# A reordered first stage: c as a row, modulation tiles between the halves of x, chunks split one by one, and products of ones in TensorE's early waits

## The reference, cut to what matters

```python
mod = (jax.nn.silu(c) @ ada_w + ada_b).reshape(bsz, DEPTH, 2, 3, D_MODEL)
shift, scale, gate = (mod[:, i, 0, k][:, None, :] for k in range(3))
h = rmsnorm(x, norm_g[i, 0]) * (1.0 + scale) + shift
# rmsnorm(x, g) = x * rsqrt(mean(x * x) + EPS) * g
b_gate, c_gate, v = jnp.split(h @ w_in, 3, axis=-1)      # a_in
u = causal_depthwise_conv(c_gate * v, conv_w)
return (b_gate * u) @ w_out                              # a_out
```

## Time and profile before

| | |
|---|---|
| time, median of 3 runs | 2176.7 us (2174.73 to 2178.79) |
| the profiled execution: its time, its span | 2175.51 us, 2173.7 us |
| TensorE busy | 2121.2 us (98%) |
| VectorE, ScalarE, POOL busy | 55%, 45%, 45% |
| TensorE idle for ScalarE's `h_hi`, whole run | 15.9 us |
| idle of TensorE before its first product | 12.9 us |
| mean granted clock | 0.998 |

### The profile page before, as it was taken

The page is one execution under the profiler, slowest core; times in us unless marked ns, Lnnn a source line. Parts: engine busy times, 40 slices in busy tenths (PEclk is TensorE's granted clock), DMA queues, the critical chain, the costliest instruction groups (busy, mean ns, idle before and its releaser), DMA issues.

```text
span 2173.7 us, 28374 instructions
## 1 busy us (share of the span) xinstructions
PE 2121.2 (98%) x10264; PEld 1720.5 (79%) x10264; DVE 1194.1 (55%) x1709; ACT 971.6 (45%) x1405; POOL 973.1 (45%) x421
## 2 busy tenths in 40 slices
PE   5999999999999999999999999999999899999998
PEld 4788888888887777778888888887776688888886
DVE  7876666412377788876422221421878745666522
ACT  5224522234455556654544333544555644444332
POOL 3544544456543333335544456564221243444563
PEclk9999999999999999999999999999999999999999
DMA  8663656733344443523233323255211132333232
GB/s 331 238 243 104 223 219 251 220 96 97 101 133 141 142 141 120 177 60 110 87 96 96 88 80 99 91 152 156 71 62 49 46 100 88 96 96 96 80 99 72
DMA packets 74477, 274.33 MB, mean 126 GB/s; under 512 B 8647, under 2 KB 11335, under 8 KB 67992
## 3 DMA queue, kind: packets, MB, share of 16 engines
q1 hardware_dynamic: 71016, 267.29, 37.7%
q10 hardware_dynamic: 3376, 5.90, 0.8%
HBM read 269.76 MB, written 8.12 MB: 128 GB/s over the span
## 4 chain that ended last, share of the span: by engine, by line
PE 73%; issue 14%; POOL 5%; DVE 5%; ACT 1%; DMA 1%; SPq 0%; ACTq 0%; POOLq 0%; DVEq 0%
PE bank L560 62%; POOL wlo L521 5%; PE bank L930 4%; PE bank L1022 2%; PE bank L951 1%; PE bank L987 1%; DVE x L1583 1%; PE bank L970 1%; PE bank L623 1%; DMA raw<-a_in_d 1%; DVE sq L1579 1%; DVE ada_first L1609 1%; PE bank L871 1%; DVE ta L1557 0%; DVE stat L1984 0%
## 5 line engine op out<-in xcount | busy, mean ns | idle before, releaser
L521 POOL TENSOR_TENSOR wlo<-raw,whi 128x1024 fp32r<-128x1024 f32 x382 | 927.7, 2436 | 1127.0 <-ACT whi L1060 1127.0
L1060 ACT ACTIVATE whi<-raw 128x1024 fp32r<-128x1024 f32 x382 | 399.8, 1055 | 570.1 <-PE bank L560 549.0
L560 PE MATMUL bank<-h_hi,whi 128*128 128x512 f32 x1608 | 630.9, 392 | 2.6 <-POOL wlo L521 2.6
L560 PE MATMUL bank<-h_hi,wlo 128*128 128x512 f32 x1608 | 626.2, 389 | 0.0
L560 PE MATMUL bank<-h_lo,whi 128*128 128x512 f32 x1608 | 625.7, 389 | 0.0
L560 PEld LDWEIGHTS bank<-h_hi,whi 128*128 128x128 f32 x1608 | 301.9, 188 | 69.6 <-issue 6.3
L560 PEld LDWEIGHTS bank<-h_hi,wlo 128*128 128x128 f32 x1608 | 301.8, 188 | 63.7
L560 PEld LDWEIGHTS bank<-h_lo,whi 128*128 128x128 f32 x1608 | 302.0, 188 | 61.7
L560 PE MATMUL bank<-g_hi,whi 128*128 128x512 f32 x592 | 230.3, 389 | 0.0
L560 PE MATMUL bank<-g_lo,whi 128*128 128x512 f32 x592 | 230.3, 389 | 0.0
L560 PE MATMUL bank<-g_hi,wlo 128*128 128x512 f32 x592 | 230.3, 389 | 0.0
(11 more groups left out here) (339 smaller groups left out, 2815.5 us busy)
## 6 DMA issues: line engine op xcount, KB each, us to landing
raw<-f_in_d SPq DMA_DIRECT2D x88, 512.0 KB, 3.6
raw<-m_d SPq DMA_DIRECT2D x65, 512.0 KB, 3.7
ada_f<-ada_d SPq DMA_DIRECT2D x24, 1024.0 KB, 6.8
raw<-g_in_d SPq DMA_DIRECT2D x44, 512.0 KB, 3.6
raw<-w_in_d SPq DMA_DIRECT2D x41, 512.0 KB, 3.6
csb<-cs_d SPq DMA_DIRECT2D x32, 640.0 KB, 5.7
ada_a<-ada_d SPq DMA_DIRECT2D x16, 1024.0 KB, 5.1
raw<-a_in_d SPq DMA_DIRECT2D x24, 512.0 KB, 6.6
```

The source lines that it names most:

```text
L521: nc.gpsimd.tensor_tensor(wlo[:, s], raw[:, s], whi[:, s].bitcast(F32), ALU.subtract).then_inc(lo_ready, 1)
L560: mm = nc.tensor.matmul(psum[bank][:], w[:, s, kk, :], xs[part == "lo"][:, k, :], start=first and kk == 0 and i == 0, stop=last and kk == ...
L1060: nc.scalar.activation(whi[:, s], raw[:, s], ACT.Copy).then_inc(hi_ready, 1)
```

## The change

It reorders the first stage; the arithmetic of all later stages stays.

- SyncE issues c first, as one row of 4 KB; then half of x, the first 160 columns of `vec`, modulation tile 0, the other half of x, `kst`, and the chunks 0 to 3 each with the tile after it. The rest of `vec` comes behind tile 7 and has a wait of its own.
- TensorE lays c over the partitions with two products of one row of ones, and ScalarE takes silu in place. A copy of silu(c) is kept in `cond` behind the last norm tile; before f_in0 this copy is copied back to PSUM in place of silu computed anew.
- The squares go to eight buffers (`y`), three sums are made of them (k = 0 to 3, 4 and 5, 6 and 7), and `token_sums` adds the three in PSUM.
- VectorE does tile 0's columns between the first and second half of the squares, tile 1's before the reciprocal; the 128 x 1 scale goes to ScalarE (`first_scale`).
- ScalarE converts chunk 0 before the root, chunk 1 after it, chunk 2 before k = 1 and chunk 3 before k = 2. POOL takes `wlo(0)`, `wlo(1)`, `h_lo(0)`, `wlo(2)`, `h_lo(1)`, `wlo(3)`, `h_lo(2)` and so on.
- TensorE takes in `four` for a_in tiles 0 and 1 first, tile 2 for k = 0 to 2 once chunk 2 is split, tile 3 likewise, and from k = 3 as before.
- `keep_warm(5, n)`, n products of 128 columns of ones to an unused bank, stand before and between the early waits.

```diff
+            sp.dma_start(cond[0:1].rearrange("p a n -> p (a n)"), io["c"]).then_inc(c_in, 16)
+            x_half(0)
+            sp.dma_start(vec[:, 0:VFIRST], io["vec"][:, 0:VFIRST]).then_inc(vec_in, 16)
             ada_start(0)
+            x_half(1)
             sp.dma_start(kst[:], io["kst"]).then_inc(kst_in, 16)
-            load(io["a_in"][0], 0)
-            ada_start(1)
-            for v in range(1, 4):
+            for v in range(4):
                 load(io["a_in"][v], v)
                 ada_start(v + 1)
             for k in range(5, KD):
                 ada_start(k)
+            sp.dma_start(vec[:, VFIRST:NV], io["vec"][:, VFIRST:NV]).then_inc(vec_in, 16)
...
+            split_lo(0)
+            for k in range(3):
+                split_lo(k + 1)
+                low_part("a_in", k)
+            for k in range(3, KD - 1):
+                low_part("a_in", k)
...
+                    turn(0, (0, 1))
+                    turn(1, (0, 1))
+                    for k in range(3):
+                        turn(k, (2,))
+                    turn(2, (0, 1))
+                    for k in range(3):
+                        turn(k, (3,))
+                    for k in range(3, KD - 2):
+                        turn(k, range(4))
...
-                pe.wait_ge(row_acc, KD - 1)
-                token_sums(4, rstd[:], True).then_inc(s_done, 1)
+                for i, k in enumerate(ROW_SUMS):
+                    pe.wait_ge(row_acc, i + 1)
+                    mm = token_sums(4, y[:, k, :], i == 0)
+                    if i == 0:
+                        keep_warm(5, 6)
+                mm.then_inc(s_done, 1)
             pe.wait_ge(const_ready, 1)
+            keep_warm(5, 8)
+            pe.wait_ge(c_in, 16)
+            for a in range(2):
+                mm = nc.tensor.matmul(psum[6 + a][:], ones[0:1, :], cond[0:1, a, :], start=True, stop=True)
+            mm.then_inc(c_rows, 1)
+            keep_warm(5, 6)
             first_root()
+            keep_warm(5, 4)
             pe.wait_ge(kst_in, 16)
             spread(4, 0, R1)
+            keep_warm(5, 6)
             four("a_in", 0)
...
+            def first_scale(k):
+                if k in (1, 2):
+                    split_hi(k + 1)
+                act.wait_ge(col_out, k + 1)
+                g = V("norm_g", k)
+                nc.scalar.activation(ncol[:, 0, 0, k:k + 1], mod[:, KD + k:KD + k + 1], ACT.Identity, bias=g, scale=g).then_inc(ncol_ready, 1)
+                act.wait_ge(ncol_ready, k + 1)
...
+            first_squares(0)
+            act.wait_ge(c_rows, 1)
+            nc.scalar.activation(silu_c, silu_c, ACT.Silu).then_inc(c_ready, 1)
             set_root()
+            first_squares(1)
+            split_hi(0)
             act.wait_ge(s_done, 1)
             take_root(0, token_sum(4))
+            split_hi(1)
             act.wait_ge(vec_in, 16)
+            mod_norm(0, "a_in", 0, first_scale)
+            act.wait_ge(c_ready, 1)
+            nc.scalar.activation(cond[:], silu_c, ACT.Copy).then_inc(c_kept, 1)
+            act.wait_ge(vec_in, 32)
...
-            condition()
+            act.wait_ge(c_kept, 1)
+            nc.scalar.activation(silu_c, cond[:], ACT.Copy).then_inc(c_ready, 1)
...
+            first_cols(0)
+            for k in (4, 6):
+                dve.wait_ge(sq_out, k + 2)
+                TT(y[:, k, :], y[:, k, :], y[:, k + 1, :], ALU.add).then_inc(row_acc, 1)
+            first_cols(1)
+            dve.wait_ge(std_out, 1)
+            nc.vector.tensor_copy(ssum[:], token_sum(4))
+            inverse(0, R1)
+            dve.wait_ge(rb_done, 1)
             for k in range(KD):
+                if k >= 2:
+                    first_cols(k)
                 scaled(k, 4, 0, "a_in")
             low("a_in")
+            dve.wait_ge(vec_in, 32)
```

More of the change, by code:

```diff
@@ L95 @@
 V0, NV = starts(VCOLS)
+VFIRST = V0["a_conv"]
 KCOLS = dict(ident=128, tri=128, qvalid=4, emask=2)
@@ L530, in splits, with low_part @@
                     split_lo(c)
+            def low_part(phase, k):
+                pool.wait_ge(in_hi, I0[phase] + k + 1)
+                nc.gpsimd.tensor_tensor(h_lo[:, k, :], tb[:, k % 2, :], h_hi[:, k, :].bitcast(F32),
+                                        ALU.subtract).then_inc(in_ready, 1)
             def low(phase):
                 for k in range(KD - 1):
[L535 to L540, removed]
+                    low_part(phase, k)
+            split_lo(0)
[4 more added lines that the diff above has]
+                low_part("a_in", k)
+            first = RING
+            for phase in BY_TILE[1:]:
                 splits(first, C0[phase] + RING)
@@ L600, in turn @@
                         lower(i, k)
-                for k in range(KD - 2):
-                    turn(k, range(4))
+                if n:
+                    for k in range(KD - 2):
+                        turn(k, range(4))
+                else:
+                    turn(0, (0, 1))
[6 more added lines that the diff above has]
+                    for k in range(3, KD - 2):
+                        turn(k, range(4))
                 turn(KD - 2, (0, 1))
@@ L1094, in x_root, with norm_out @@
                 take_root(X_ROOT[i], token_sum(4))
-            def norm_out(i, phase, a, b):
+            def norm_out(i, phase, a, b, ahead=None):
                 for k in range(KD):
-                    if i == 0:
-                        act.wait_ge(ncol_ready, k + 1)
+                    if ahead is not None:
+                        ahead(k)
                     act.wait_ge(t_out, KD * i + k + 1)
@@ L1140, in y_tile, with first_squares @@
                 split_hi(c + RING + chunks - 1)
[L1142 to L1155 removed]
+            def first_squares(h):
+                act.wait_ge(x_in[h], 16)
+                for k in range(4 * h, 4 * h + 4):
+                    nc.scalar.activation(y[:, k, :], x[:, k, :], ACT.Square).then_inc(sq_out, 1)
+            def first_scale(k):
[5 more added lines that the diff above has]
+                act.wait_ge(ncol_ready, k + 1)
+            act.wait_ge(const_ready, 1)
+            nc.scalar.activation(root[:, SPARE, 1:2], epscol[:], ACT.Silu)
+            first_squares(0)
+            act.wait_ge(c_rows, 1)
+            nc.scalar.activation(silu_c, silu_c, ACT.Silu).then_inc(c_ready, 1)
             set_root()
+            first_squares(1)
+            split_hi(0)
             act.wait_ge(s_done, 1)
             take_root(0, token_sum(4))
[L1159 to L1160 removed]
+            split_hi(1)
             act.wait_ge(vec_in, 16)
[L1162 removed]
+            mod_norm(0, "a_in", 0, first_scale)
+            act.wait_ge(c_ready, 1)
+            nc.scalar.activation(cond[:], silu_c, ACT.Copy).then_inc(c_kept, 1)
+            act.wait_ge(vec_in, 32)
             for j in range(8):
@@ L1619, in first_cols @@
             def first_cols(k):
[L1621 to L1625, removed]
+                dve.wait_ge(first_in[k], 16)
+                mod_col(k, ada_first[k][:, 0])
+                mod_col(KD + k, ada_first[k][:, 1]).then_inc(col_out, 1)
             def scale_col(q):
```

33 lines of the change are left out of this document (12 added, 21 removed).

## The result

The changed kernel takes 2170.9 us (median of 12 runs, 2169.8 to 2172.7) beside 2176.8 for the kernel before (12 runs, 2174.7 to 2179.0): the ratio is 0.9973, 95% interval 0.9966 to 0.9981. The forecast was 2171.9 in a range from 2169.2 to 2175.4. The profiled execution has a span of 2168.3 us, before 2173.7.

What follows compares the result with a forecast made beforehand. Only the program's start could be shortened, held by the fourth chunk's transfer, then VectorE. Reordering ends the first four tiles at 48.2 instead of 53.05 us, a gain of 4.8 from the 2176.7 median: 2171.9 us, range 2169.2 to 2175.4.

Steps and rivals of the forecast that it cites:

- What holds the start: First stage before the change: the fourth weight chunk's transfer until 26.2, then VectorE at 3.59 us a k.
- the sum: First stage: tile 1 at 15.9, root spread at 19.9, h_lo(2) at 30.8, then 76 products to 48.2; gain 4.8 us.
- the first and third step: First stage: tile 1's arrival at 15.9 us, and the root, spread at 19.9 with TensorE at its high level.
- the POOL step: POOL's list h_lo(0), wlo(2), h_lo(1), wlo(3), h_lo(2), fed from 22.1 us and ending at 30.8.
- the mark: End of the first four tiles, where the table product starts: 53.05 us before, 48.2 predicted; its gain passes to the span.
- The level: TensorE's clock, 1.2 or 2.4 GHz, taken as high from the spread on: spread 1.1 us instead of 2.05.
- the low level stays: Rival: spread or first tiles at 1.2 GHz, costing 1.0 and 1.8 us; gain 2.0 to 3.8, about 2173.8; chance 0.18.
- Bursts of ones: Products of ones in TensorE's early waits cost nothing; before the spread 1.1 us, 2.05 if low, of 2.4 available.
- The 128x1 operation: On VectorE it waits for POOL; moving it cuts VectorE's period from 3.59 to 3.11 us and costs ScalarE 0.3.
- the copies of c: TensorE's 128 copies of c, ready between 7.3 and 9.3 us, hide under the squares but for 0.3.
- table loads: f_in0's loop: 22 more loads, 28.2 us of ScalarE, costing nothing; rival up to 23.4 us slower, chance 0.04.
- the end of vec: The rest of vec arrives by 35 us, is wanted at 43, and costs nothing.

Runs made afterwards that it cites:

- e1: Changed kernel without its 30 products of ones: 2171.8 us, ratio 0.9972 to 0.9991.
- e6: Changed kernel with modulation tile 0 transferred behind the second half of x instead of between the halves: 2175.2 us, single run.
- e11: Changed kernel plus a 512 KB copy of c's row to 128 partitions, behind the first half of x: 2174.8 us, single run.
- e7: Changed kernel with the root's reciprocal between tile 1's two columns on VectorE: 2169.6 us, single run.
- e4: Changed kernel with all four chunks split before the first norm tile, as in the old order: 2175.3 us, ratio 0.9985 to 1.0005.
- e2: Kernel before plus products of ones alone, 24 before the row sums and 36 behind the spread: 2176.5 us, single run.
- c0: Changed kernel run once more with no edit: 2169.5 us, single run.
- e9: Changed kernel with the reciprocal between tile 1's columns and products of ones in the waits for h_lo(0) and h_lo(1): 2171.2 us, ratio 0.9958 to 0.9983.
- e10: Changed kernel with the silu table loaded ahead of f_in0: 2172.3 us, ratio 0.9969 to 0.9988.
- e3: Changed kernel with the 128x1 scale back on VectorE behind each pair of columns: 2174.3 us, single run.
- e8: Changed kernel with three and six products of ones in TensorE's waits for h_lo(0) and h_lo(1): 2173.2 us, single run.
- e5: Changed kernel plus c's row copied to 127 partitions, behind the first half of x: 2197.5 us, single run.

## Why the prediction was right, and where it was not

**What holds the start.** Right, but for its last release. The order was the one in the sum: tile 1, its two columns, the root, one norm tile, POOL's list. The sum has POOL's fifth instruction, h_lo(2), release 76 products; in both traces of the changed kernel the last wait of TensorE ends with the third, h_lo(1), and 86 products follow without one, from 26.90 to 48.22. The low level is why (below). In e1 and e6 to e11 TensorE does wait for h_lo(2), 1.0 to 1.7 us, as the sum has it. e11 and e7 move the first and third step, e4 the POOL step, and each moves the mark; e2, in the kernel before, leaves its chain alone and gives nothing.

**The terms.** Tile 1 was 0.34 earlier than taken (15.56 for 15.9) and this carried through to h_lo(2), 30.42 for 30.8. From there to the mark it was 17.8 for 17.4. Both errors are 0.4 and of opposite sign: that the mark agrees to 0.02 us is partly luck.

**The level.** The forecast had it high from the spread on. It was high at the spread (1.13) and low again from 26.90 to 30.34, after waits of 0.88 and 1.68; the table by stretch for 27 to 30.5 us has a granted clock of 0.51, 1.2 GHz:

```profile
27.00:30.50 3.50, 3.50 (x9) 2.73 (x10) 3.04 (x6) 3.10 (x6) 3.50 (x3) 0.51 1.02 431
```

This was a part of the rival "the low level stays", and its price was 0.3 us (17.80 and, in c0, 17.79, less the 17.5 of e1 and of e6 to e11, where the products from h_lo(1) on are high) and not 1.8. The 86 products did take 1.8 longer than at 0.227 each (21.32 beside 19.5), but at the high level TensorE would have been at h_lo(2) by 29.2 and waited for POOL until 30.42. What I had against that rival was a misreading: I took four records in 0.92 behind the wait of 3.14 for the high level. Four of them take 0.63 at the high level, as in the changed kernel's timeline of TensorE:

```profile
1698.91 0.63 PE L1008 MATMUL bank<-kst,ta 128*128 128x128 f32 x4 [3.14 <-ACT pt L1484]
```

and 1.09 in e6, whose next big products stand 0.43 apart (1711.30 and 1711.73):

```profile
1700.82 1.09 PE L1008 MATMUL bank<-kst,ta 128*128 128x128 f32 x4 [3.14 <-ACT pt L1484]
```

The same wait leaves either level behind it, by execution: 0.63 or 0.64 in five traces, 0.92 and 0.94 in the kernel before and in e1, 1.09 in seven. I should have compared four records with four, and not with a figure halved from eight.

**Bursts of ones.** That they cost nothing was right for the changed kernel, where the burst before the spread has ended when the root is ready. In e6 it was low (1.94), was still running, and held the spread 0.8 us. That the bursts bring the spread to the high level holds in 7 of the 11 traces that have them (1.11 to 1.13 in both of the changed kernel, e4, e6, e7, e9 and e10). In e3, e11 and e8 the spread took 1.47, 1.59 and 1.88; TensorE had waited 3.48, 1.87 and 1.79 before it, and at most 1.19 before the seven others. In e5 it took 1.53, 5.3 us after a wait of 24.85.

**The 128x1 operation.** That it waits for POOL, and leaves VectorE with a period of 3.0 (3.11 predicted), was right. In the sum its removal stood as 0.48 a round, read from rows of 0.56; but those were waits for POOL as well, and alone it takes 0.16. Its worth beside the other edits was 4.36 us, a price that the prediction doesn't have, since it never asked what the operation would do on VectorE in the new order.

**ScalarE, the copies of c, table loads, the end of vec.** All at no cost, as predicted. The 128x1 operation takes 0.37 to 0.39 on ScalarE (0.3 taken), and the copy that keeps silu stands at 41.07 with 3.39 us of waiting behind it.

**The size of the total.** The mark gives 4.83; the medians differ by 5.9 (2176.8 less 2170.9) with an interval from 4.1 to 7.4 (0.0019 to 0.0034 of 2176.8). The prediction set the total on the gain of the mark, and that lies inside. The other 1.1 are of the size of the attention stage's scatter, and without a trace of each run they can't be told from it. That the forecast is 1.0 from the median follows from them, and is no test of the mark.

**Parts don't add up.** Taken out one at a time, the parts are worth 0.9 (ones), 4.4 (128x1), 2.5 (interleaving), 2.0 (c's bytes) and 2.3 (tile 0 between the halves), 12.1 together, where all of them bring 4.8. Without the 128x1 edit VectorE's period is the bound again, without the interleaving the fourth chunk's conversion. In e1, e6 and e11 the chain is the same one, longer.

## What to carry to other kernels

Follow the start of a program as one chain over the engines, and price an edit by the step of it that moves: the same 128x1 operation was 0.16 us of work and 4.4 us of the end. Where VectorE and POOL both read SBUF, look for small VectorE instructions of two SBUF inputs that last as long as POOL's, and move them to ScalarE or ahead of POOL's list. When the gain is a few microseconds, compare a landmark behind the edit in the traces before the totals.

## What the runs showed of the hardware

- A VectorE instruction of 128x1 with two inputs in SBUF took 2.21 and 2.33 us beside POOL's splits, 0.55 to 0.56 beside the end of a POOL instruction, and 0.16 with POOL idle; two 128x512 sums took 3.44 together, 0.69 each alone.
- A broadcast of 4 KB rows to 127 partitions moved 25 to 29 GB/s and held the next issue of the queue for 10.46 us; to 128 partitions its issue took 0.43.
- TensorE's first twelve or so microseconds were at the low level in the changed kernel though it was busy 11.87 of 13.00 us; in e6 the c products were already high at 4.48 (1.98 for the four, 3.78 in the changed kernel). After the waits of 0.88 and 1.7 in the first stage the level fell in both traces of the changed kernel (26.90) and held in e6, e7 and e10, whose waits are the same to 0.03. The granted clock printed 1.00 for 0 to 13 us all the same, but 0.51 for the low stretch at 27: in the first stretch only the spacing tells.
- TensorE's level in the stretch behind one wait of 3.14 us goes with up to 4.1 us of a 2170 us run: attention stages of 414.25 us at a granted clock of 1.00 and of 418.35 at 0.66. The first four records behind the wait don't tell it alone: they were low in e7 (1.09), whose stage took 415.77, and high in e2 (0.64), whose stage took 416.17.
